# Attention with its scores issued three heads ahead, a weight split placed behind it, and two residuals that multiply by the gate first

## The reference, cut to what matters

```python
# attention of layer 1: 8 heads of 128, causal over 256 tokens
q, k, v = split(x @ w_qkv, 3); q, k = rope(q), rope(k)
p = softmax(q @ k.T * 128 ** -0.5 + causal)
h = (p @ v) @ w_out
# residuals of the last two parts of block two
def rmsnorm(x, g): return x * rsqrt(mean(x * x) + EPS) * g
new_lat = h_lat + gt_l * rmsnorm(out_l, g_post)                # n = 2, behind w_out
return h + 0.5 * gate * rmsnorm(swiglu_2(u, w13, w2), g_post)  # n = 3, the last
# what follows n = 2: modulate(rmsnorm(new_lat, g_pre), shift, scale)
```

## Time and profile before

| what | us |
|---|---|
| median of 3 runs (1765.05 to 1772.45) | 1765.84 |
| the profiled execution: its own time | 1767.61 |
| its span in the profile | 1765.7 |
| busy in it: TensorE / VectorE / ScalarE / GpSimd | 1687.6 / 950.8 / 765.0 / 156.3 |

### The profile page before, as it was taken

The page is one execution under the profiler, slowest core; times in us unless marked ns, Lnnn a source line. Parts: engine busy times, 40 slices in busy tenths (PEclk is TensorE's granted clock), DMA queues, the critical chain, the costliest instruction groups (busy, mean ns, idle before and its releaser), DMA issues.

```text
span 1765.7 us, 27650 instructions
## 1 busy us (share of the span) xinstructions
PE 1687.6 (96%) x11886; PEld 1544.3 (87%) x11886; DVE 950.8 (54%) x1091; ACT 765.0 (43%) x975; POOL 156.3 (9%) x160
## 2 busy tenths in 40 slices
PE   7999999999898799999999999999999999989998
PEld 6996878998776579998999899989889999979996
DVE  4664236554634465545755565556776364665543
ACT  4453333443334434443444344444655444444442
POOL 0113420000000000001100130012100020120000
PEclk8999999999999999999999999999999999999999
DMA  7553248665556677655765566545535233576652
GB/s 227 149 186 120 96 122 260 188 179 190 185 189 215 215 219 211 191 189 177 188 176 190 180 182 188 172 169 186 166 120 167 72 115 113 190 229 178 182 186 85
DMA packets 329167, 306.54 MB, mean 174 GB/s; under 512 B 11953, under 2 KB 286934, under 8 KB 328918
## 3 DMA queue, kind: packets, MB, share of 16 engines
q1 hardware_dynamic: 324246, 296.19, 54.6%
q10 hardware_dynamic: 4528, 7.54, 1.3%
q0 software_dynamic: 272, 1.05, 0.2%
HBM read 303.69 MB, written 1.05 MB: 173 GB/s over the span
## 4 chain that ended last, share of the span: by engine, by line
PE 87%; DVE 6%; ACT 3%; DMA 2%; issue 2%; POOL 1%; SPq 0%; DVEq 0%; POOLq 0%; ACTq 0%
PE ps L412 48%; PE ps L436 17%; PE ps L455 8%; ACT whi L383 2%; PE ps L473 1%; DVE wlo L389 1%; PE ps L1178 1%; PE ps L1194 1%; PE ps L594 1%; PE ps L1785 1%; DMA raw<-in_b_w_qkv 1%; PE ps L2323 1%; PE ps L2222 1%; DVE x L708 1%; DVE small L663 0%
## 5 line engine op out<-in xcount | busy, mean ns | idle before, releaser
L389 DVE TENSOR_TENSOR wlo<-raw,whi 128x2048 fp32r<-128x2048 f32 x247 | 567.7, 2300 | 412.5 <-ACT whi L383 412.1
L412 PE MATMUL ps<-ah,whi 128*128 128x256 f32 x2368 | 677.9, 286 | 7.1 <-DVE wlo L389 7.1
L412 PE MATMUL ps<-al,whi 128*128 128x256 f32 x2368 | 672.6, 284 | 0.0
L412 PE MATMUL ps<-ah,wlo 128*128 128x256 f32 x2368 | 672.5, 284 | 0.0
L383 ACT CAST whi<-raw 128x2048 fp32r<-128x2048 f32 x247 | 470.1, 1905 | 245.5 <-PE ps L436 157.1
L412 PEld LDWEIGHTS ps<-ah,whi 128*128 128x128 f32 x2368 | 455.9, 193 | 10.2 <-issue 7.1
L412 PEld LDWEIGHTS ps<-al,whi 128*128 128x128 f32 x2368 | 456.0, 193 | 1.8 <-issue 1.4
L412 PEld LDWEIGHTS ps<-ah,wlo 128*128 128x128 f32 x2368 | 455.9, 193 | 0.0
L764 ACT ACTIVATE f_sig<-ps 128x256 f32<-128x256 f32 x110 | 42.2, 383 | 358.8 <-PE ps L412 345.1
L436 PE MATMUL ps<-whi,fh 128*128 128x512 f32 x440 | 171.5, 390 | 0.0
L436 PE MATMUL ps<-whi,fl 128*128 128x512 f32 x440 | 171.2, 389 | 0.0
(11 more groups left out here) (355 smaller groups left out, 1642.8 us busy)
## 6 DMA issues: line engine op xcount, KB each, us to landing
raw<-in_f_w SPq DMA_DIRECT2D x132, 512.0 KB, 4.6
raw<-in_w_a SPq DMA_DIRECT2D x132, 512.0 KB, 4.3
raw<-in_w_ada SPq DMA_DIRECT2D x72, 512.0 KB, 4.5
raw<-in_w_in SPq DMA_DIRECT2D x68, 512.0 KB, 4.5
raw<-in_w_b SPq DMA_DIRECT2D x66, 512.0 KB, 4.6
raw<-in_a_w_in SPq DMA_DIRECT2D x32, 512.0 KB, 5.2
raw<-in_b_w_qkv SPq DMA_DIRECT2D x24, 512.0 KB, 5.0
raw<-in_a_w_out SPq DMA_DIRECT2D x8, 512.0 KB, 4.1
```

The costliest lines, as they stand in the source:

```text
L389: dve.tensor_tensor(wlo[:, c % RING, :], raw[:, r % RING, :], whi[:, c % RING, :].bitcast(F32), ALU.subtract).then_inc(S("lo_ready"), 1)
L412: last = pe.matmul(out_ap, a, b, start=(i == 0), stop=(i == n - 1))
```

## The change

In the attention, `HEADS_AHEAD` is 3: three buffers of `a_s` and its sums, three heads of scores ahead of the first transposes, two heads of maxima ahead of the head in hand. The last split of `m_qkv`'s steps, which is that of chunk 2 of `m_out`, goes from ahead of the attention to behind its last heads, on ScalarE between the outputs of heads 6 and 7, and on VectorE behind the last probabilities; the eight `w_ada` chunks are loaded ahead of chunk 2 of `m_out` and no longer ahead of chunk 3. Six of eight `w_ada` chunks are multiplied one head later or more. `lo_part` goes from VectorE to GpSimd. `values(7)` goes ahead of chunk 0 of `m_out`. In the copies to `a_t`, block 6 goes a step earlier and block 7 ahead of the copies to `a_v`.

In the residuals n = 2 and 3, VectorE multiplies the product by the gate first, once the squares of that half are taken (`res_gate_dve`), and then does row factor and addition in one operation (`res_add_dve`). The mean goes into the squares as a scale, so that GpSimd adds eps to the first half's sum alone and early (`res_first_pool`; in all four residuals). For n = 2 the squares of the new rows are taken in halves (`rms_half`), between the squares of the product.

```diff
-                    ("m_out", 3): range(20, 28), ("up1", 2): range(28, 31), ("up1", 4): [31],
+                    ("m_out", 2): range(20, 28), ("up1", 2): range(28, 31), ("up1", 4): [31],
...
+    HEADS_AHEAD = 3
     a_qk = at("a_qk", 0, [P, TT, 2048])
     a_v = at("a_v", 16, [P, TT, D])
     a_t = at("a_t", 24, [P, 16, T])
     a_rope = at("a_rope", 40, [P, 4, 16, 16])
-    a_s = at("a_s", 44, [P, 2, 384])
-    a_pt = at("a_pt", 47, [P, 2, 384])
-    a_o = at("a_o", 50, [P, 2, T])
-    a_max = sm(4).rearrange("p (s t) -> p s t", s=2)
-    a_sum = sm(4).rearrange("p (s t) -> p s t", s=2)
+    a_s = at("a_s", 44, [P, HEADS_AHEAD, 384])
+    a_pt = at("a_pt", 48.5, [P, 2, 384])
+    a_o = at("a_o", 51.5, [P, 2, T])
...
-    BLOCKS_AT = {9: (0, 1, 2), 10: (3, 4, 5), 11: (6, 7)}
+    BLOCKS_AT = {9: (0, 1, 2), 10: (3, 4, 5, 6), 11: (7,)}
...
+            if j == q.n - 1:
+                qk_turn_act(act, 7)
             if j % 2:
                 act.wait_ge(*S("used", c + 1))
                 for tt in range(TT):
                     i = 512 * (j // 2)
                     dst = a_v[:, tt, i - 2048:i - 1536] if j >= 8 else a_qk[:, tt, i:i + 512]
                     act.copy(dst, ps[q.bank[j - 1 + tt]][:, :]).then_inc(S("taken_a"), 1)
-            for n in BLOCKS_AT.get(j, ()):
-                qk_turn_act(act, n)
-            cut_ahead(act, c)
+            if j < q.n - 1:
+                for n in BLOCKS_AT.get(j, ()):
+                    qk_turn_act(act, n)
+                cut_ahead(act, c)
...
+            if j < q.n - 1:
+                cut_ahead(dve, c)
...
-        scores(0)
-        scores(1)
+        for h in range(HEADS_AHEAD):
+            scores(h)
         ada_chunk_pe(pe, 20)
         ada_chunk_pe(pe, 21)
         for h in range(8):
             turned(h)
-            if h < 6:
-                scores(h + 2)
-                ada_chunk_pe(pe, 22 + h)
+            if h + HEADS_AHEAD < 8:
+                scores(h + HEADS_AHEAD)
+            if 1 <= h <= 5:
+                ada_chunk_pe(pe, 21 + h)
             if h == 4:
                 ada_cols_pe(pe, 5)
             if h == 7:
-                ada_cols_pe(pe, 6)
-                pe.wait_ge(*S("scored", 7))
-                pe.wait_ge(*S("pt", 7))
-                pe.wait_ge(*S("o_lo", 4))
-                stream_pe(pe, "m_out", ah, al, only=[0])
+                ada_chunk_pe(pe, 27)
             values(h)
+        pe.wait_ge(*S("scored", 7))
+        pe.wait_ge(*S("pt", 7))
+        pe.wait_ge(*S("o_lo", 4))
+        stream_pe(pe, "m_out", ah, al, only=[0])
+        ada_cols_pe(pe, 6)
...
-            if h in (3, 6):
-                ada_row_act(act, 4 + h // 3)
+            if h == 3:
+                ada_row_act(act, 5)
+        cut_ahead(act, segs["m_qkv"].cut[11])
         out_parts(7)
+        ada_row_act(act, 6)
...
-            wait_from(dve, *S("pt_ps", h - 1))
+            wait_from(dve, *S("pt_ps", h - HEADS_AHEAD + 1))
...
         maxima(0)
+        maxima(1)
         for h in range(8):
-            if h < 7:
-                maxima(h + 1)
+            if h < 6:
+                maxima(h + 2)
             probs(h)
-            if h:
-                lo_part(dve, h - 1)
             if h == 5:
                 ada_sum_dve(dve, 5)
-        lo_part(dve, 7)
+        cut_ahead(dve, segs["m_qkv"].cut[11])
         ada_sum_dve(dve, 6)
-    def lo_part(dve, h):
-        dve.wait_ge(*S("o_hi", h + 1))
-        dve.tensor_tensor(al[:, h, :], a_o[:, h % 2, :], ah[:, h, :].bitcast(F32), ALU.subtract)\
+    def lo_part(pool, h):
+        pool.wait_ge(*S("o_hi", h + 1))
+        pool.tensor_tensor(al[:, h, :], a_o[:, h % 2, :], ah[:, h, :].bitcast(F32), ALU.subtract)\
...
-                       accum_out=res_ss[:, tt, h:h + 1]).then_inc(S("res_sq"), 1)
+                       scale=ROOT_D, accum_out=res_ss[:, tt, h:h + 1]).then_inc(S("res_sq"), 1)
...
         res_square(act, 0, 1)
+        rms_half(act, 0, 0)
         act.wait_ge(*used(q.name, q.n - 1))
         res_square(act, 1, 1)
+        rms_half(act, 0, 1)
+        rms_half(act, 1, 0)
+        rms_half(act, 1, 1)
+    def rms_half(act, tt, h):
+        half = slice(512 * h, 512 * h + 512)
+        act.wait_ge(*S("res", 4 + 2 * tt + h + 1))
+        act.activation(xn[:, tt, half], x0[:, tt, half], ACT.Square, scale=ROOT_D,
+                       accum_out=rms_hs[:, tt, h:h + 1]).then_inc(S("rms_sq"), 1)
...
+    def res_first_pool(pool, n, tt):
+        pool.wait_ge(*S("res_sq", 4 * n + (tt + 1 if n == 2 else 2 * tt + 1)))
+        pool.tensor_scalar(res_ss[:, tt, 0:1], res_ss[:, tt, 0:1], EPS, None, ALU.add).then_inc(S("res_a"), 1)
+    def res_root_pool(pool, n, tt):
+        r = res_rn[:, tt:tt + 1]
+        pool.wait_ge(*S("res_sq", 4 * n + (4 if tt else 3 if n == 2 else 2)))
+        pool.wait_ge(*S("res_a", 2 * n + tt + 1))
+        pool.tensor_tensor(r, res_ss[:, tt, 0:1], res_ss[:, tt, 1:2], ALU.add).then_inc(S("res_m"), 1)
+        pool.wait_ge(*S("res_m", 2 * n + tt + 1))
+        pool.tensor_tensor(r, r, half_neg[:, 0:1], ALU.pow).then_inc(S("res_rn"), 1)
...
+            res_first_pool(pool, n, tt)
+            if n != 2:
+                res_root_pool(pool, n, tt)
+        if n == 2:
+            for tt in range(TT):
+                res_root_pool(pool, n, tt)
+                rms_half_pool(pool, tt)
...
+    def res_gate_dve(dve, n, i, tt, h):
+        half = slice(512 * h, 512 * h + 512)
+        dve.wait_ge(*S("res_sq", 4 * n + i + 1))
+        dve.tensor_tensor(xn[:, tt, half], ffn_banks(tt, h), gb[:, 0, half], ALU.mult).then_inc(S("res_scaled"), 1)
+    def res_add_dve(dve, n, tt, scaled, x, sem):
+        dve.wait_ge(*S("res_rn", 2 * n + tt + 1))
+        dve.wait_ge(*S("res_scaled", 4 * n + scaled))
+        for h in range(2):
+            half = slice(512 * h, 512 * h + 512)
+            dve.scalar_tensor_tensor(x[:, tt, half], xn[:, tt, half], res_rn[:, tt:tt + 1], x[:, tt, half],
+                                     ALU.mult, ALU.add).then_inc(S(sem), 1)
+    def res_late_dve(dve, n, x, sem):
+        dve.wait_ge(*S("gate_row", 2 * n + 2))
+        if n == 2:
+            res_gate_dve(dve, n, 0, 0, 0)
+            res_gate_dve(dve, n, 1, 1, 0)
+            res_gate_dve(dve, n, 2, 0, 1)
+            res_add_dve(dve, n, 0, 3, x, sem)
+            res_gate_dve(dve, n, 3, 1, 1)
+        else:
+            res_gate_dve(dve, n, 0, 0, 0)
+            res_gate_dve(dve, n, 1, 0, 1)
+            res_gate_dve(dve, n, 2, 1, 0)
+            res_add_dve(dve, n, 0, 2, x, sem)
+            res_gate_dve(dve, n, 3, 1, 1)
+        res_add_dve(dve, n, 1, 4, x, sem)
...
-        rms_act(act, 4, x0, "res", 5)
...
-        res_dve(dve, 2, x0)
+        res_late_dve(dve, 2, x0, "res")
...
-        res_dve(dve, 3, x0)
+        res_late_dve(dve, 3, x0, "res_half")
...
+        for h in range(8):
+            lo_part(pool, h)
...
-        rms_pool(pool, 4)
...
```

More of the change, by code:

```diff
@@ L42 @@
 NEG = -1e30
-N_SMALL = 740
+N_SMALL = 748
 ARENA = 78
@@ L1617, in att_pe @@
     def att_pe(pe):
-        pe.wait_ge(*evicted("m_qkv", 11))
         def scores(h):
@@ L1637, in turned @@
                 last = pe.transpose(ps[6][:, i * P:i * P + P] if h % 2 == 0 else
-                                    ps[7][:, i * P:i * P + P], a_s[:, h % 2, i * P:i * P + P], ident)
+                                    ps[7][:, i * P:i * P + P], a_s[:, h % HEADS_AHEAD, i * P:i * P + P], ident)
             last.then_inc(S("pt_ps"), 1)
         def values(h):
+            if h == 0:
+                pe.wait_ge(*evicted("m_qkv", 11))
             pe.wait_ge(*S("pt", h + 1))
@@ L1681, in exps @@
             for tt, c in ((0, slice(0, P)), (1, slice(P, 384))):
-                act.activation(a_s[:, h % 2, c], a_s[:, h % 2, c], ACT.Exp,
-                               bias=a_max[:, h % 2, tt:tt + 1], accum_out=a_sum[:, h % 2, tt:tt + 1])\
+                b = h % HEADS_AHEAD
+                act.activation(a_s[:, b, c], a_s[:, b, c], ACT.Exp,
+                               bias=a_max[:, b, tt:tt + 1], accum_out=a_sum[:, b, tt:tt + 1])\
                    .then_inc(S("exps"), 1)
@@ L1891, in build @@
     res_rn, rms_ss = sm(2), sm(2)
+    rms_hs = sm(4).rearrange("p (t h) -> p t h", t=2)
+    ROOT_D = float(D ** -0.5)
     def res_square(act, tt, h):
         act.activation(xn[:, tt, 512 * h:512 * h + 512], ffn_banks(tt, h), ACT.Square,
-                       accum_out=res_ss[:, tt, h:h + 1]).then_inc(S("res_sq"), 1)
+                       scale=ROOT_D, accum_out=res_ss[:, tt, h:h + 1]).then_inc(S("res_sq"), 1)
     def res_act(act, q):
@@ L1910, in res_out_act @@
         res_square(act, 0, 1)
+        rms_half(act, 0, 0)
         act.wait_ge(*used(q.name, q.n - 1))
         res_square(act, 1, 1)
+        rms_half(act, 0, 1)
[16 more added lines that the diff above has]
+        pool.tensor_tensor(r, r, half_neg[:, 0:1], ALU.pow).then_inc(S("res_rn"), 1)
     def res_pool(pool, n, x=None):
         for tt in range(TT):
```

(32 more changed lines are left out.)

19 lines of the change are left out of this document (11 added, 8 removed).

## The result

| | median us | runs | 
|---|---|---|
| before | 1767.93 | 4, 1765.05 to 1772.45 |
| changed | 1748.95 | 4, 1747.60 to 1750.00 |

The ratio is 0.9899, 95% interval 0.9874 to 0.9925: 17.8 us off (13 to 22); the two medians differ by 19.0. I had forecast 1755.5, within 1752.5 to 1760.8. The profiled execution took 1749.66, its span is 1747.9.

What follows compares the result with a forecast made beforehand. TensorE is busy nearly throughout, so only its waits can give time back; the attention is a chain with no engine full. Attention -10.4, residual behind `w_out` +1.6, last residual -1.5: -10.3 from median 1765.84 gives 1755.5 us, range 1752.5 to 1760.8.

Steps and rivals of the forecast that it cites:

- Start of the attention: Ahead of head 0: first mask at 569.9, not 573.5; first transposes at 574.7, 2.3 us early.
- One head: Attention, heads 0 to 5: with the output split on GpSimd, a head takes 3.48 us against 4.38, at full clock.
- last heads: Heads 6 and 7 into `m_out`: TensorE sets the pace, 2.4 then 1.8 us; `m_out` goes on 10.4 us early.
- GpSimd's splits: Eight output splits in the attention: 0.5 to 0.6 us each, bounds 0.3 and 1.3, ending before VectorE's next scaling; cost nothing.
- Rival 1: GpSimd's splits collide with VectorE's scalings in each head, 0.6 us each over seven heads, 4.2 us: 1759.7; chance 0.20.
- Loads: Weight loads during the attention's heads, `w_ada` and chunk 2 of `m_out`: costed at nothing.
- Residual behind `w_out`: Residual after `w_out`: the new order on ScalarE, GpSimd and VectorE makes the block behind 1.6 us late, bounds 0.8 to 2.4.
- Residual at the end: Last residual: GpSimd has two operations, not three, and the last add ends 1.5 us early, bounds 0.9 and 2.1.
- The sum: Whole kernel: -10.4 + 1.6 - 1.5 = -10.3 us, taken from the median 1765.84 to give 1755.5 us.
- The range: Whole kernel: 1752.5 to 1760.8 us for 8 in 10, up to rival 1.

Runs made afterwards that it cites:

- the split in front: Changed kernel with the split of chunk 2 of `m_out` ahead of the attention again and its load ahead of `w_ada`'s: 1755.16 us, 0.9942.
- Both runs on its causes: Changed kernel with `lo_part` back on VectorE, 1758.97 us; changed kernel with two buffers and scores two heads ahead, 1747.63 us.
- the second comparison: Both kernels run again without edit: before 1766.86 us, changed 1751.52 us, ratio 0.9927.
- The fill runs: Kernel before with unused identity products in TensorE's attention pauses, 24 ahead of the first scores, 8 or 4 behind each head's product but the last: 1765.04 and 1762.43 us.

## Why the prediction was right and where it failed

**Start of the attention: right, a little short.** Counted from the last product of `m_qkv`, the first mask comes 4.05 earlier (forecast 3.6) and the first transposes 2.7 (forecast 2.3). The forecast let block 7's copy start where the two copies had started, behind those to `a_v`; it starts ahead of them, 0.5 earlier. With the split in front nothing is left of it (6.47 against 6.52), so the weight split's move decides it; whether the move would give as much with the copies in the old order was not run.

**One head and last heads: right.** 3.48 measured, 3.48 forecast; 2.41 and 1.83 against 2.4 and 1.8; 7.9 against 8.1 from the last transposes to `m_out` going on. From the last product of `m_qkv` to `m_out` going on it was 47.83 and is 36.62: 11.2 against the forecast 10.4. Both runs on its causes agree: the split's place is worth 5.6 us and up to 1.6 more by the clock, the third buffer nothing.

**GpSimd's splits: right in effect, short in size.** 0.73 for seven of them, not 0.5 to 0.6, within the bounds, and 2.14 for the last. Rival 1's collision would have begun 0.17 us later; I had thought 0.3. Loads cost nothing, as forecast.

**Residual behind `w_out`: right in mechanism, too dear.** 1.0 lost, not 1.6 (F 23.2 to 24.25). The three gate products took 1.88 where I had 2.14, so that every later step came 0.3 earlier, and GpSimd's operations and the adds behind them gave the other 0.3. The order is the cause: undone, it gives 1.76.

**Residual at the end: right.** 1.66 gained, 1.5 forecast.

**The sum: the step that failed.** The stretches that the change touches gave 11.2 - 1.0 + 1.7 = 11.9 us, and I had 10.3. The rest of the 17.8 (12.9 in the second comparison) lies where the sum had zero. The step that failed is "the difference is one of absolute microseconds, so I take it from the median": it took every other stretch, and the old kernel's clock, as equal in all executions. Between the first profiles of the two kernels (spans 1765.7 and 1747.9), counted at the same products of TensorE, the 17.8 us are 4.1 up to the last product of `m_qkv` (A, where before has low stretches at 518.6 and 545.9 us and is back at 66.1 in its next profile), 11.2 in the attention, -0.8 from there to the mLSTM stage, 2.6 in E, -1.0 in F and 1.7 in G. So 5.9 of them are terms that the sum did not have. They are in part chance, and that the measured time came out below the range by 3.5 us is in part luck of the executions as well.

Within C the sum had the old kernel wrong too. "One head" says: that pause shrinks, so I count the full clock. I did so for the new kernel and took the old one from a profile whose C was nearly at the full clock, 41.61. Other executions of before take 44.52 and 45.49 in C, since the clock falls a second time, behind the last heads, and chunk 0 of `m_out` takes 7.5 us and not 5.3 ("Last heads" has 5.47 for it). In the seven profiles with the new heads it never falls there. That is 2.3 us on the mean. The fill runs support the clock as the cause in C; in E it is seen by the rows, not tested.

**What stays open.** E is 391.3 to 393.4 in all five profiles with the old attention and 388.2 to 388.7 in seven of eight with the new one, D 193.9 or 194.0 in three of five and 192.5 in all eight, though neither stage was touched. Its length goes with the low stretches in it: the seven short ones have a low clock at one place, the six long ones at two or three, in some of them for twice as long. The eighth E of the new attention, 392.9, shows that the changed code can fall into it as well. Whether the shorter front of the program makes the falls in E rarer, or eight profiles flatter it, isn't settled; a change of the kernel's start by a few microseconds of idle time would tell, and wasn't tried. By the two comparisons the change is worth 13 to 18 us, of which 11.9 follow from its order and about 2.3 from the clock in C.

**The range.** 8.3 us wide, it held the terms of the sum and nothing of the executions. Before alone spreads from 1759 to 1773. To hold both medians of the changed kernel, 1748.95 and 1751.52, its low end had to lie 4 us lower, near 1748.

## What to carry to other kernels

In a chain between engines that work in order, look for the instruction that waits for the last round while it stands ahead of the next round's first one: moving that one (0.43 us of work) to an idle engine gave 0.9 us a round, and the deeper buffer nothing. Put the work of the old round's tail ahead of the new round's head on every engine that serves both, or a factor that is needed first is made last (here 1.76 us). And before a sum is made against one profile, see in two or three which stretches keep their length: a pause can cost more than its idle time, if the clock falls in it and the work behind is TensorE's (7.5 us for 5.3 here), or nothing more, if that work waits for another engine.

## What the runs showed of the hardware

- The same pause with the same work around it (3.45 busy of 5.00 us) had a granted clock of 1.00 in one execution and 0.77 in another: a pause makes a fall possible, not certain. The same stage took 388.6 us with the clock low at one place of it, and 392.9 with three.
- GpSimd's subtraction of 128x256 took 0.73 us, and 2.14 when it began under VectorE's of 128x2048; VectorE's kept its 2.29.
- A product of the 128x128 identity in fp32 by itself was two instructions and 0.22 us (1.79 us for eight products, 16 instructions).
